# Expert order in a top-2 mixture of experts: smallest experts behind the five fixed ones, the largest last

## The reference

```python
g_sel = jnp.argmax(g_logit, axis=-1)                       # one group of 4
e_logit = take_along_axis(e_logit, g_sel)                  # its 8 experts
top_p, top_i = lax.top_k(jax.nn.softmax(e_logit), TOP_K)   # two of them
gates = g_w[:, None] * top_p / jnp.sum(top_p)
hid = jax.nn.silu(xb @ w_eg[e]) * (xb @ w_eu[e])           # 1024 -> 256
out = hid @ w_ed[e]                                        # 256 -> 1024
y = jnp.einsum('nkd,nk->nd', y_slot, gates)
```

## Time and profile before

| | us |
|---|---|
| median of 3 runs | 2698.16 |
| lowest and highest run | 2690.39, 2700.79 |
| the profiled execution | 2689.56 |
| its span, first to last instruction | 2687.7 |
| PE busy (share of the span) | 2392.2 (89%) |
| VectorE busy | 1149.1 (43%) |
| ScalarE busy | 709.4 (26%) |
| GpSimd busy | 369.5 (14%) |

### The profile page before, as it was taken

The page is one execution under the profiler, slowest core; times in us unless marked ns, Lnnn a source line. Parts: engine busy times, 40 slices in busy tenths (PEclk is TensorE's granted clock), DMA queues, the critical chain, the costliest instruction groups (busy, mean ns, idle before and its releaser), DMA issues.

```text
span 2687.7 us, 37671 instructions
## 1 busy us (share of the span) xinstructions
PE 2392.2 (89%) x15472; PEld 1395.9 (52%) x15472; DVE 1149.1 (43%) x2152; ACT 709.4 (26%) x1452; POOL 369.5 (14%) x523
## 2 busy tenths in 40 slices
PE   7999997899999968998599999888999999599964
PEld 4644555666666643333365455555566675333323
DVE  3245556743232353332351555575422332633325
ACT  2123444432111331111401244533311032211113
POOL 0003323310000001111100132161100000011111
PEclk9999998899999979999799999988989999699997
DMA  5001001152232148999510100013521311799965
GB/s 173 18 18 28 12 5 36 41 200 82 92 136 87 63 190 312 412 423 405 221 35 4 33 18 6 4 37 122 196 71 40 136 71 63 279 369 415 422 280 193
DMA packets 80715, 386.19 MB, mean 144 GB/s; under 512 B 20638, under 2 KB 27420, under 8 KB 61276
## 3 DMA queue, kind: packets, MB, share of 16 engines
q1 hardware_dynamic: 62380, 304.92, 29.6%
q0 software_dynamic: 17568, 76.57, 7.4%
q10 hardware_dynamic: 576, 2.10, 0.2%
HBM read 352.42 MB, written 40.36 MB: 146 GB/s over the span
## 4 chain that ended last, share of the span: by engine, by line
PE 71%; DVE 11%; issue 5%; PEld 4%; ACT 4%; DMA 2%; POOL 1%; PEldq 1%; POOLq 0%; SPq 0%; DVEq 0%; ACTq 0%
PE ps L707 13%; PE ps L1363 12%; PE ps L1387 6%; PE ps L1277 4%; PE ps L765 4%; PE ps L845 4%; PEld ps L707 4%; PE ps L857 2%; PE ps L873 2%; PE ps L1043 2%; PE ps L823 2%; PE ps L1349 2%; PE ps L976 1%; DVE nmax L1954 1%; DVE arena L2053 1%
## 5 line engine op out<-in xcount | busy, mean ns | idle before, releaser
L707 PE MATMUL ps<-arena,ring 128*128 128x352 f32 x1704 | 509.7, 462 | 1.9 <-ACTq L459 1.0
L707 PEld LDWEIGHTS ps<-arena,ring 128*128 128x128 f32 x1704 | 325.6, 191 | 183.7 <-issue 5.0
L1363 PE MATMUL ps<-arena 128*32 128x512 f32 x2304 | 322.5, 614 | 25.6 <-issue 19.9
L2496 DVE COPY arena<-ps 128x1024 f32<-128x1024 f32 x44 | 53.9, 1224 | 342.6 <-PE ps L1349 342.6
L1363 PEld LDWEIGHTS ps<-arena 128*32 128x32 f32 x2304 | 93.3, 113 | 195.2 <-issue 195.2
L1387 PE MATMUL ps<-arena 128*32 128x512 f32 x1408 | 160.2, 595 | 3.8 <-ACT arena L1765 3.8
L845 PE MATMUL ps<-arena 96*128 96x512 f32 (+3 forms) x384 | 146.1, 490 | 0.0
L2635 POOL DMA_INDIRECT arena<-xrow,arena x46 | 47.2, 1026 | 600.8 <-DVE arena L2471 322.1
L1535 ACT ACTIVATE ring<-ps 128x512 f32<-128x512 f32 (+2 forms) x192 | 87.1, 490 | 123.8 <-PE ps L857 123.8
L1277 PE MATMUL ps<-arena,ring 128*128 128x352 f32 x384 | 117.7, 463 | 1.6 <-DVE arena L2329 1.6
L1043 PE MATMUL ps<-consts,arena 128*128 128x128 f32 x640 | 99.4, 295 | 19.4 <-ACT arena L1650 10.4
(11 more groups left out here) (436 smaller groups left out, 3620.7 us busy)
## 6 DMA issues: line engine op xcount, KB each, us to landing
arena<-in_w_gu SPq DMA_DIRECT2D x52, 2048.0 KB, 14.2
arena<-in_w_dn SPq DMA_DIRECT2D x64, 1024.0 KB, 12.2
ring<-in_ring SPq DMA_DIRECT2D x56, 512.0 KB, 3.6
ring<-in_w_gu SPq DMA_DIRECT2D x12, 2048.0 KB, 13.5
arena<-yrow SPq DMA_DIRECT2D x16, 1024.0 KB, 7.6
arena<-in_mem_k SPq DMA_DIRECT2D x16, 512.0 KB, 7.1
arena<-in_mem_v SPq DMA_DIRECT2D x16, 512.0 KB, 10.1
xrow<-arena SPq DMA_DIRECT2D x16, 512.0 KB, 7.8
```

The source lines that it names most:

```text
L707: mm = pe.matmul(ps[:, (j % 2) * NCH + c, 0:CH], ring[:, j // per, (j % per) * units + k, :], src[:, k, tok], start=k == k0, stop=k == uni ...
L1363: mm = pe.matmul(ps[r, 2 + n % 2, :], xb_t[:, n % 2, k, r], w_gu[e % NW][:, k, :], start=k == 0, stop=k == KT - 1, skip_group_check=True)
L2496: dve.tensor_copy(xb_t[:, n % 2, :, :], xt_ps).then_inc(tx_evac, 1)
```

## The change

The order of ranks 5 to 31 is turned round. `GROUPS` now has the five fixed experts, then nine ranks of two groups, then 17 of three, then one of four. Counts are compared the other way, so the smallest of the 27 has rank 5 and the largest rank 31; the tie constants follow, and the fixed five get large negative ones so that they stay first. The formulas for `cap` and `base` are rewritten for the new shape, with one VectorE instruction more. No other line is changed; the loops and waits that are derived from `GROUPS` follow.

```diff
-GROUPS = [r for r, n in enumerate([3] * NW + [4] + [3] * 17 + [2] * 9) for _ in range(n)]
+GROUPS = [r for r, n in enumerate([3] * NW + [2] * 9 + [3] * 17 + [4]) for _ in range(n)]
...
-    tie = [65536 * (NW - e) if e < NW else NE - 1 - e for e in range(NE)]
+    tie = [65536 * (e - NW) if e < NW else e for e in range(NE)]
...
-                step(dve.tensor_tensor(beats, key.unsqueeze(1).broadcast_to([P, NE, NE]), key.unsqueeze(2).broadcast_to([P, NE, NE]), ALU.is_gt))
+                step(dve.tensor_tensor(beats, key.unsqueeze(1).broadcast_to([P, NE, NE]), key.unsqueeze(2).broadcast_to([P, NE, NE]), ALU.is_lt))
                 step(dve.tensor_reduce(place, beats, AX, ALU.add))
-                step.mark(dve.tensor_scalar(cap, place, float(NW), float(GRP), ALU.is_equal, ALU.mult))
-                step.mark(dve.tensor_scalar(jump, place, float(NW + 18), float(GRP), ALU.is_ge, ALU.mult))
-                step.mark(dve.tensor_scalar(base, place, float(NW), float(GRP), ALU.is_gt, ALU.mult))
-                step(dve.tensor_scalar(nov, place, -float(NW + 18), 0.0, ALU.add, ALU.max))
-                step.mark(dve.scalar_tensor_tensor(out=cap, in0=cap, scalar=float(3 * GRP), in1=jump, op0=ALU.add, op1=ALU.subtract))
-                step(dve.scalar_tensor_tensor(out=base, in0=place, scalar=float(3 * GRP), in1=base, op0=ALU.mult, op1=ALU.add))
-                step.mark(dve.scalar_tensor_tensor(out=base, in0=nov, scalar=-float(GRP), in1=base, op0=ALU.mult, op1=ALU.add))
+                step.mark(dve.tensor_scalar(cap, place, float(NE - 1), float(GRP), ALU.is_ge, ALU.mult))
+                step.mark(dve.tensor_scalar(jump, place, float(NW), float(GRP), ALU.is_ge, ALU.mult))
+                step.mark(dve.tensor_scalar(base, place, float(NW + 9), float(GRP), ALU.is_ge, ALU.mult))
+                step(dve.tensor_scalar(nov, place, -float(NW), 0.0, ALU.add, ALU.max))
+                step.mark(dve.scalar_tensor_tensor(out=cap, in0=cap, scalar=float(3 * GRP), in1=base, op0=ALU.add, op1=ALU.add))
+                step(dve.tensor_scalar(nov, nov, 9.0, -float(GRP), ALU.min, ALU.mult))
+                step.mark(dve.tensor_tensor(cap, cap, jump, ALU.subtract))
+                step(dve.scalar_tensor_tensor(out=base, in0=place, scalar=float(3 * GRP), in1=nov, op0=ALU.mult, op1=ALU.add))
```

## The result

| | before | after |
|---|---|---|
| median, us | 2694.92 (12 runs) | 2713.91 (12 runs) |
| lowest and highest | 2687.29, 2700.79 | 2703.98, 2720.53 |
| profiled execution (its span) | 2689.56 (2687.7) | 2716.21 (2714.3) |

The ratio of after to before is 1.0065, with a 95% interval from 1.0049 to 1.0080: slower by 19 us. The predicted time was 2706 with a range of 2692 to 2721; the time lies inside, but the outcome held likeliest (within 0.5% of before, chance 0.72) is not the one that came: 0.65%, with an interval that begins at 0.49%. Before took 277.0 and 276.6 us for its two stages, after 283.4 and 282.4.

A forecast was written before the change was run, and what follows sets the result against it. Bound per layer by PE for 19 blocks and the weight stream for three; 3.4 (layer 1) + 3.9 (layer 2) + 0.4 (routing) = 7.7 us on 2698.16 gives 2706, range 2692 to 2721 (forecast's own 2700 to 2712).

The forecast's parts named there:

- 12 experts and 9 blocks of rows, 44.5 MB: What the stream must bring by block 18, layer 1, after rank 16's weights: 105.5 us at 422 GB/s.
- Just in time: Block 18, layer 1: rank 28's weights land at 1243.3, PE is ready at 1244.6, so no wait.
- e13: Expert of rank 13, needed by block 7: lands 16.7 us later at 1110.0; a wait of 3.3 us.
- e16: Expert of rank 16, needed by block 9: issued near 1124.8, 13 us to land, a wait of 2.7 us.
- three times 1.72: Clock loss of 1.72 us for each slow gate/up after the waits at blocks 6, 7 and 9.
- The tail from block 21's start: Block 21's start to last down: 18.75 us before, 17.0 after at full clock; layer 2 gives back 1.33 instead of 1.72.
- Rival 1: Blocks 9 to 18 starve too: at 410 GB/s about +3.4 us more per layer, 14.5 in all; chance 0.22.
- Rival 2: Early stretch lacks loads, not bandwidth; earlier issue helps blocks 6, 7, 9: 2691, or 2668 without waits; chance 0.10.
- Rival 3: Bytes decide: block 21 starts at the last weight's landing, 1274 in both orders; tail gains 1.7 per layer, 2695; chance 0.13.
- clock rival: Expert blocks: the sum if every step waiting for a DMA starts at the lower clock; no size or chance given.
- The routing's price of 0.22 us: One more dependent VectorE instruction on 32 columns ahead of the expert stage: +0.2 us per layer.
- the absence of overflow blocks: Expert stage: none run now, and with the same capacities per size rank none will; no cost.

The follow-up runs named there:

- e3: The changed kernel with half of each expert's gate and up weights not loaded and the loaded half used twice: 2680.3 us, ratio to before 0.9947.
- e7: The changed kernel with down weights of rank r - 2 instead of r - 1 loaded behind gate/up weights of rank r: 2710.8 us, ratio to before 1.0048.
- e6: The kernel before with down weights of rank r - 2 instead of r - 1 loaded behind gate/up weights of rank r: 2696.9 us, ratio 0.9994.

## Why the prediction was right, and where it was not

**Place and kind: right.** The gaps stood before blocks 5, 6, 7 and 9, for gate/up weights, and blocks 19 to 21 had none. Block 21 ran at full clock. Blocks counted from the start of block 1, since block 0's gate/up varies by itself:

| start of, from block 1 | forecast | after, four layers |
|---|---|---|
| block 6 | 65.8 | 66.1 to 66.4 |
| block 7 | 82.5 | 81.8 to 84.6 |
| block 10 | 123.7 | 122.8 to 125.5 |
| block 21 | 252.2 | 254.5 to 254.7 |

**The size: 3.65 us a layer in the stage were forecast, 7.0 measured.** That the time lies in the range owes something to its width, for the forecast's own range ended at 2712. Three terms of the sum were off.
- "12 experts and 9 blocks of rows, 44.5 MB" and "Just in time": the margin of 1.3 us at block 18 was not there. Nine blocks in before, 9 to 17, moved 44.52 MB, as the forecast says. In after the stretch from block 9 to block 18, from the landing of rank 16 to that of rank 28, took 108.6 us and moved 46.05 MB. What moved there, before first, then after (the DMA view of 1120.94 to 1226.06 and of 1146.49 to 1255.07: packets, MB, share; q1 is SyncE's weights, q0 GpSimd's rows):

```profile
q1 hardware_dynamic: 3419, 37.29, 83.9%
q0 software_dynamic: 2612, 7.07, 17.0%
...
q1 hardware_dynamic: 3559, 38.82, 84.4%
q0 software_dynamic: 2601, 7.08, 16.4%
```

  The rows are the same, 0.79 MB a block against the 0.75 taken, so the larger experts at the end are not the reason. The 12 experts are 37.75 MB, and 38.82 MB of weights came: 1.07 MB belong to loads issued behind rank 28's (the down weights of rank 27 and a part of rank 29's gate/up), which moved beside them. The forecast let a load land as soon as all that was issued up to it had moved. The 1.5 MB in all are 3.6 us at 424 GB/s. In layer 2 the part was smaller (45.49 MB in 107.4 us). Over the four layers of the two profiles the gaps from block 12 to 18 came to 0.5 to 2.8 us.
- "16.7 us" to e13 and 13 us to land for e16: the early stream was taken at 422 GB/s. From block 4 to block 9 it ran at 393 and 401. The prediction had seen that SyncE's wait for a down holds e16, and had not asked the same of e13, which e3 and e7 then showed. That block 10 came out near was luck in part: the gaps up to block 9 add up to 13.2 to 15.5 us where 13.4 were forecast, and the slow gate/ups cost 3.6 to 4.4 us where three times 1.72 were.
- The tail from block 21's start, 18.75 us before (the rows give 18.71) and 17.0 after: the difference is 0.7 us on average instead of 1.5. Before's slow block 21 was in two layers of six. A loss at the clock in a single profile was booked as a property of the kernel.

Block 21 came 254.6 us behind block 1 on average, 2.4 later than the forecast's 252.2. In before it stands 246.4 behind block 1 on average, 0.7 less than the 247.1 from which the prediction counted. The tail adds 0.8, and block 0, whose gate/up varies by itself, took 0.5 less in after. 2.4 + 0.7 + 0.8 - 0.5 = 3.4, which is the difference of 7.0 and 3.65.

**The rivals.** Rival 1 had the size (14.5 us and more) and in layer 1 its sign, gaps before blocks 12, 15 and 18, but not the cause: the three-group part moved 423 to 425 GB/s, no 410, and lost 0.5 to 2.8 us to gaps, none of them with a clock loss. Rival 2's reading of the 352 GB/s of the earlier trace rows, that loads were missing and not bandwidth, was right for the stretch, as e6 shows with 423; its gain was not, since the change makes the loads scarcer there. Rival 3 is out: block 21 did not wait for its weights. The "clock rival below" of which the prediction speaks is not in its list; the clock stands in the forecast and in rival 1. The routing's price of 0.22 us (after: 995.33 to 996.18 from the first dependent step to `excess`, 0.85 us, before 0.65) and the absence of overflow blocks were right.

Behind the first two blocks, a gate/up after a gap of up to 1.9 us ran at full pitch in all 14 profiles (7.07 us), one after a gap of 3.2 us or more never did (8.4 to 10.0 us), and of the 18 after gaps from 2.0 to 3.1 us five took 8.77 us. The forecast gave its gap of 2.7 us a loss, and rival 1 even one of 1.7: too strict. The Trainium skill (TensorE: Matmul & The Clock Gate, section HAM oscillation) describes a loop whose every step waits some 3 to 5 us for a DMA and then starts at the lower clock; the trace agrees for gaps of that length, from 3.20 to 4.76 us.

## What to carry to other kernels

Where a stream of weights is nearly as slow as the engine that uses it, try the hungriest stretch last: an early hole is followed by work of fixed pace that wins nothing back, while the stream of weights then runs out before the end (190 GB/s in block 20 of the changed kernel's layer 1 and 54 in block 21). All this was seen in one kernel with one set of rows. Before a bandwidth is put into a sum, ask whether the queue is full at that point: follow each load to the wait that releases it and to what stands ahead of it in its issuing queue, for a gap of the engine also delays those releases. And take no clock loss of one execution for a term; compare two profiles of the same kernel first.

## What the runs showed of the hardware

The stretch outside the stages is the same program in all of these kernels but for up to seven instructions in each routing, and took 2134 to 2158 us in 14 profiles, whatever the order. Part of it is in one place. TensorE in the attention of layer 2, from the first to the last of its blocks, in before, in after and in e2 (half the loads, before's order):

```profile
1544.10:1748.90 204.80, 185.33 (x1303) 114.88 (x1301) 111.55 (x290) 101.58 (x239) 57.25 (x45) 1.00 0.04 9
```

```profile
1560.30:1771.50 211.20, 191.67 (x1303) 118.87 (x1301) 111.67 (x290) 101.96 (x239) 57.36 (x45) 0.97 0.04 9
```

```profile
1541.60:1752.70 211.10, 191.61 (x1303) 119.32 (x1301) 111.57 (x290) 101.94 (x239) 57.25 (x45) 0.97 0.04 9
```

With the same instructions, the granted clock is 1.00 in one and 0.97 in the others, and 6.4 us go with it, a third of what the change cost. e2 has before's order, so it isn't the change. In the 14 profiles the score matmuls of that attention (L845 in before) took from 198.3 us at 1.00 to 207.8 at 0.95, and those of layer 1 the same, with short and long ones in both orders. Among executions of one kernel the time is 2.4 us shorter for each 0.001 more of mean granted clock (0.9438 on average for before, 0.9418 for after). What decides whether that stretch keeps its clock stays open, and with it whether the 3 us left over above lie there.

DMA held 422 to 425 GB/s of weights, gathers and scatters on one core over stretches of 16 to 117 us in both orders. A busy share near 1 did not tell that this was reached: the windows of after stand at 0.97 to 1.00 with 385 to 399 GB/s.
